# Gated units of a four-layer float32 block: two pairs of column groups as sets of four chunks with 30 block products for 32, and Silu on ScalarE

## The reference

```python
def swiglu(x, w_gate, w_up, w_down):
    return (jax.nn.silu(x @ w_gate) * (x @ w_up)) @ w_down
...
def _swiglu(h, w_gate_up, w_down):
    gu = h @ w_gate_up
    g, u = gu[..., :D_FF], gu[..., D_FF:]
    return (jax.nn.silu(g) * u) @ w_down
```

## Time and profile before

| | |
|---|---|
| median of 3 runs | 1240.11 us (1239.87 to 1241.81) |
| the profiled execution, its own time | 1240.0 us |
| its span, first to last instruction | 1238.2 us |
| TensorE busy | 1225.8 us, 99% of the span |
| VectorE busy | 928.7 us, 75% |
| ScalarE busy | 705.9 us, 57% |
| GpSimd busy | 89.3 us, 7% |
| granted clock of TensorE | 1.00 |

### The profile page before, as it was taken

The page is one execution under the profiler, slowest core; times in us unless marked ns, Lnnn a source line. Parts: engine busy times, 40 slices in busy tenths (PEclk is TensorE's granted clock), DMA queues, the critical chain, the costliest instruction groups (busy, mean ns, idle before and its releaser), DMA issues.

```text
span 1238.2 us, 16107 instructions
## 1 busy us (share of the span) xinstructions
PE 1225.8 (99%) x6318; PEld 1021.4 (82%) x6318; DVE 928.7 (75%) x1293; ACT 705.9 (57%) x1065; POOL 89.3 (7%) x121
## 2 busy tenths in 40 slices
PE   7999999999999999999999999999999999999998
PEld 6778888888888888888888888888888888888887
DVE  7995767698788766778887756676888785666787
ACT  7765654455898644455687535444456644544452
POOL 2410000000100100000232000000001300000000
PEclk9999999999999999999999999999999999999999
DMA  8344545555554565555554224545455315555452
GB/s 308 106 137 148 188 171 204 187 187 203 192 201 159 197 213 197 174 189 212 183 200 170 69 103 169 205 170 204 170 204 187 132 35 204 204 173 199 172 183 89
DMA packets 32539, 216.63 MB, mean 175 GB/s; under 512 B 3904, under 2 KB 4544, under 8 KB 7376
## 3 DMA queue, kind: packets, MB, share of 16 engines
q1 hardware_dynamic: 30384, 210.32, 48.6%
q0 software_dynamic: 1360, 4.78, 1.2%
q10 hardware_dynamic: 720, 0.50, 0.1%
HBM read 214.54 MB, written 1.05 MB: 174 GB/s over the span
## 4 chain that ended last, share of the span: by engine, by line
PE 93%; DVE 4%; issue 1%; DMA 1%; ACT 0%; SPq 0%; DVEq 0%; ACTq 0%
PE PS L484 26%; PE PS L486 26%; PE PS L485 26%; PE PS L490 6%; PE PS L860 2%; PE PS L884 1%; PE PS L521 1%; PE PS L519 1%; PE PS L518 1%; PE PS L567 1%; PE PS L562 1%; PE PS L561 1%; DVE WL L1838 1%; DVE YG L2215 1%; DMA X<-in_x 1%
## 5 line engine op out<-in xcount | busy, mean ns | idle before, releaser
L1838 DVE TENSOR_TENSOR WL<-RAW,WH 128x2048 fp32r<-128x2048 f32 (+3 forms) x200 | 434.1, 2174 | 182.3 <-ACT WH L1199 182.3
L1199 ACT ACTIVATE WH<-RAW 128x2048 fp32r<-128x2048 f32 (+3 forms) x200 | 364.4, 1824 | 262.2 <-PE PS L486 262.1
L484 PE MATMUL PS<-WH,HTh 128*128 128x512 f32 (+1 forms) x848 | 334.6, 395 | 0.8 <-DVE WL L1838 0.6
L486 PE MATMUL PS<-WH,HTl 128*128 128x512 f32 (+1 forms) x848 | 329.0, 388 | 0.0
L485 PE MATMUL PS<-WL,HTh 128*128 128x512 f32 (+1 forms) x848 | 328.3, 387 | 0.0
L486 PEld LDWEIGHTS PS<-WH,HTl 128*128 128x128 f32 x848 | 159.2, 188 | 33.3
L484 PEld LDWEIGHTS PS<-WH,HTh 128*128 128x128 f32 x848 | 159.4, 188 | 32.7 <-DVE WL L1838 1.7
L485 PEld LDWEIGHTS PS<-WL,HTh 128*128 128x128 f32 x848 | 159.5, 188 | 30.6
L484 PE MATMUL PS<-WH,YAh 128*128 128x512 f32 x354 | 139.9, 395 | 0.1
L486 PE MATMUL PS<-WH,YAl 128*128 128x512 f32 x354 | 138.0, 390 | 0.0
L485 PE MATMUL PS<-WL,YAh 128*128 128x512 f32 x354 | 137.8, 389 | 0.0
(11 more groups left out here) (446 smaller groups left out, 1737.6 us busy)
## 6 DMA issues: line engine op xcount, KB each, us to landing
RAW<-in_w SPq DMA_DIRECT2D x196, 1024.0 KB, 4.9
BC<-in_rows POOLq DMA_DIRECT2D x4, 512.0 KB, 4.1
YG<-in_mem POOLq DMA_DIRECT2D x4, 512.0 KB, 5.0
X<-in_x SPq DMA_DIRECT2D x2, 512.0 KB, 5.4
RAW<-in_w SPq DMA_DIRECT2D x4, 256.0 KB, 5.7
BC<-in_s SPq DMA_DIRECT2D x1, 512.0 KB, 11.6
YG<-in_s SPq DMA_DIRECT2D x1, 512.0 KB, 11.9
BB<-in_s SPq DMA_DIRECT2D x1, 512.0 KB, 12.5
```

The costliest lines, as they stand in the source:

```text
L484: e.matmul(out, ah, bh, start=start, stop=False, skip_group_check=joined)
L486: return e.matmul(out, al, bh, start=False, stop=stop, skip_group_check=joined)
L1199: e.activation(WH[:, c % NW, w], RAW[:, c % NR, w], ACT.Copy).then_inc(S.hi, 1)
L1838: e.tensor_tensor(WL[:, c % NW, w], RAW[:, c % NR, w], WH[:, c % NW, w].bitcast(f32), SUB).then_inc(S.lo, 1)
```

## The change

In each unit the pairs 2 and 3, and 6 and 7, become sets of four chunks. A chunk of a set holds two tiles of k for both pairs of column groups (1024 columns). The first and third of a set are plain, eight products each over four banks; the second and fourth have seven products, with sums of weights (from RAW, as in the down projection, but kept in `TGh`, `TGl`, which lie in YB) and sums of activations, made once per unit from the unit's input (`forms`, buffers GSh and GSl). Eight additions per set join the results before the gates of both pairs. Pairs get banks by a table (`BANKS`). The gate function is Silu of ScalarE for Tanh, so VectorE has one instruction per row tile and the factors 0.5 go; an Exp of two columns ends the ScalarE part of the first three units. The order of all three engines around the sets is written anew (`ahead`, `column_set`, `group`). The diff, cut:

```diff
 NF = len(FAST)
+SETS = (2, 6)
+NS = 2 * len(SETS)
+BANKS = ((0, 1), (6, 7), (0, 2), (1, 3), (6, 7), (2, 3), (0, 2), (1, 3), (6, 7), (0, 1), (6, 7))
...
+    def half(k, nk, g):
+        return ("pair", gate, up, lead, k, nk, 256 * g, uo + 256 * g)
     for g in range(11):
-        for k in (0, 4):
-            out.append([("pair", gate, up, lead, k, 4, 256 * g, uo + 256 * g)])
+        if g in SETS:
+            for k in (0, 2, 4, 6):
+                if k in (2, 6):
+                    out.append([half(k, 1, g + 1), half(k, 1, g), half(k + 1, 1, g), half(k + 1, 1, g + 1)])
+                else:
+                    out.append([half(k, 1, g), half(k, 1, g + 1), half(k + 1, 1, g), half(k + 1, 1, g + 1)])
+        elif g - 1 not in SETS:
+            out += [[half(0, 4, g)], [half(4, 4, g)]]
     for ci in range(11):
...
                 out += [sb(key + n, [128, NF, 384], f32r) for n in ("SFh", "SFl")]
...
+        TGh, TGl = (a[:, 0:8, :].rearrange("p (n a) c -> p n (a c)", a=2) for a in (YBh, YBl))
         SR = JK[:, :].rearrange("p (b c) -> p b c", b=2)
...
+        def joined(f, n):
...
+            def early_chunk(f, a, first, c):
+                m, i = FASTS[c], 0 if first else 1
+                GSh, GSl = FB[f][8:10]
+                k = 2 if first else 6
...
+                def mul(b, x, w, own):
+                    return mm3(PS[:, b, :], *x, *w, own and first, not first)
...
+                def top_left():
+                    return mul(5, Y(0, 0), W(1), True)
+                def with_sums():
+                    e.wait_ge(S.tlo, 4 * m + 1)
+                    mul(6, S_(1), T(1), True).then_inc(S.tu, 1)
+                    e.wait_ge(S.tlo, 4 * m + 2)
+                    if first:
+                        e.wait_ge(S.ylo, fold_n(f, a - 2))
+                    mul(4, S_(0), T(0), True).then_inc(S.tu, 1)
+                e.wait_ge(S.lo, c + 4)
+                e.wait_ge(S.gsl, 2 * f + i + 1)
+                if first:
+                    side(0, Y(1, 0), W(2))
+                    side(1, S_(3), W(3))
+                    e.wait_ge(S.an, gt_n(f, a - 1, 1))
+                    with_sums()
+                else:
+                    top_left().then_inc(S.ms, 1)
+                    with_sums()
+                    side(0, Y(1, 0), W(2))
+                    side(1, S_(3), W(3))
+                e.wait_ge(S.tlo, 4 * m + 3)
+                mul(7, S_(2), T(2), True).then_inc(S.tu, 1)
+                e.wait_ge(S.tlo, 4 * m + 4)
+                tk = mul(2, Y(1, 1), T(3), False)
+                if first:
+                    e.wait_ge(S.ylo, fold_n(f, a - 1))
+                    tk = top_left()
+                tk.then_inc(S.used, 1)
+            def set_mm(f, a, cs, folds):
+                def plain(c, k0):
+                    e.wait_ge(S.lo, c + 4)
+                    for t in range(2):
+                        if k0 == 0:
+                            e.wait_ge(S.an, gt_n(f, a - 1 if a > 2 and t else a - 2, 1))
+                        for k in (k0, k0 + 1):
+                            for half in range(2):
+                                o = (k % 2) * 1024 + half * 512
+                                tk = product(c, PS[:, 2 * t + half, :], (HTh, HTl), k, t, slice(o, o + 512), k == 0,
+                                             k == 5 and t == 1 and half == 1)
+                    tk.then_inc(S.used, 1)
+                plain(cs[0], 0)
+                folds()
+                early_chunk(f, a, True, cs[1])
+                plain(cs[2], 4)
+                early_chunk(f, a, False, cs[3])
...
-                edge_mm(cs[0:2], 4, 512, FPAIRS[0], ed)
-                for g in range(1, 11):
-                    def freed(k, t):
-                        if k == 0 and g > 2:
-                            e.wait_ge(S.an, gt_n(f, g - 3, t))
-                    rows_mm(cs[2 * g:2 * g + 2], 4, 8, 512, (HTh, HTl), FPAIRS[g % 3], freed)
-                    fold(g - 1)
+                def free(g, t):
+                    if g - 2 in SETS:
+                        e.wait_ge(S.cb, set_joins(f, g - 2) + (6 if t else 1))
+                    elif g == 5:
+                        e.wait_ge(S.an, gt_n(f, 3, 1))
+                    elif g == 9:
+                        e.wait_ge(S.an, gt_n(f, 7, 1))
+                    elif g == 10:
+                        e.wait_ge(S.an, gt_n(f, 8, t))
+                def group(g):
+                    for n, c in enumerate(cs[2 * g:2 * g + 2]):
+                        e.wait_ge(S.lo, c + 4)
+                        for t in range(2):
+                            if n == 0:
+                                free(g, t)
+                            for k in range(4 * n, 4 * n + 4):
+                                w = slice(512 * (k % 4), 512 * (k % 4) + 512)
+                                tk = product(c, PS[:, BANKS[g][t], :], (HTh, HTl), k, t, w, k == 0, k == 7)
+                        tk.then_inc(S.used, 1)
+                edge_mm(cs[0:2], 4, 512, BANKS[0], ed)
+                group(1)
+                fold(0)
+                set_mm(f, 2, cs[4:8], lambda: fold(1))
+                group(4)
+                fold(2)
+                fold(3)
+                group(5)
+                fold(4)
+                set_mm(f, 6, cs[12:16], lambda: fold(5))
+                group(8)
+                fold(6)
+                fold(7)
+                group(9)
+                fold(8)
+                group(10)
+                fold(9)
                 wide_mm(cs[22:], ed + 1, lambda k: ydst(f, k), lambda ci: e.wait_ge(S.ylo, fold_n(f, 9 if ci == FAST[0] else ci)), lambda: fold(10), 1, f)
...
                 m = FASTS[c]
-                e.wait_ge(S.used, c - 1)
+                dst = TGh if early(c) else TSh
+                e.wait_ge(S.used, c - 4 if early(c) and m % 2 == 0 else c - 1)
                 for q, n in enumerate(T_ORDER):
                     e.wait_ge(S.tr, 4 * m + (2, 3, 3, 4)[q])
-                    copy(TSh[:, n, :], TR_[:, n, :]).then_inc(S.thi, 1)
+                    copy(dst[:, n, :], TR_[:, n, :]).then_inc(S.thi, 1)
...
-                    e.wait_ge(S.used, cs[2 * g + 1] + 1)
+                    p = BANKS[g]
+                    if g in SETS or g - 1 in SETS:
+                        a = g if g in SETS else g - 1
+                    else:
+                        a = None
+                        e.wait_ge(S.used, cs[2 * g + 1] + 1)
                     if g == 0:
-                        e.wait_ge(S.rsx, f + 1)
+                        e.wait_ge(S.rs, RSTD[f"row{ed}"])
                     for t in range(2):
                         if g > 1:
-                            e.wait_ge(S.sg, gt_n(f, g - 2, t))
-                        e.activation(TH[:, g % 2, t, :], PS[:, p[t], 0:256], ACT.Tanh, scale=st[:, 4 + t:5 + t]).then_inc(S.th, 1)
+                            e.wait_ge(S.an, gt_n(f, g - 2, t))
+                        if a is not None:
+                            e.wait_ge(S.cb, set_joins(f, a) + (8 if t else 3 + g - a))
+                        e.activation(TH[:, g % 2, t, :], PS[:, p[t], 0:256], ACT.Silu, scale=st[:, 2 + t:3 + t]).then_inc(S.th, 1)
                 def fold(g):
                     hi, lo, j = ydst(f, 2 * g)
...
+                def forms():
+                    for i in range(2):
+                        e.wait_ge(S.gs, 8 * f + 4 * i + 4)
+                        copy(FB[f][8][:, i, :], (JK[:, 512:1024], FB[f][5][:, 2, :])[i]).then_inc(S.gsh, 1)
+                def group(g, *folds):
+                    feed(cs[2 * g])
+                    feed(cs[2 * g + 1])
+                    for g_ in folds:
+                        fold(g_)
+                    tanh(g)
+                def ahead(a):
+                    g = a - 1
+                    sums_hi(cs[2 * a + 1])
+                    feed(cs[2 * g])
+                    fold(g - 1)
+                    tanh(g)
+                    feed(cs[2 * g + 1])
+                def column_set(a):
+                    feed(cs[2 * a])
+                    fold(a - 1)
+                    sums_hi(cs[2 * a + 3])
+                    feed(cs[2 * a + 1])
+                    n = SETS.index(a)
+                    e.wait_ge(S.ms, 9 * f + 3 * n + 1)
+                    copy(FB[f][5][:, 2, :], PS[:, 5, :]).then_inc(S.eo, 1)
+                    feed(cs[2 * a + 2])
+                    tanh(a)
+                    tanh(a + 1)
+                    feed(cs[2 * a + 3])
                 edge_mm(cs[0:2], ed)
                 tanh(0)
-                for g in range(1, 11):
-                    feed(cs[2 * g])
-                    feed(cs[2 * g + 1])
-                    fold(g - 1)
-                    tanh(g)
-                    if beside:
-                        beside(g)
+                forms()
+                ahead(2)
+                column_set(2)
+                group(4, 2, 3)
+                if beside:
+                    beside(1)
+                    beside(2)
+                ahead(6)
```

(78 more changed lines are left out.)

72 lines of the change are left out of this document (45 added, 27 removed).

## The result

The changed kernel takes 1305.31 us (median of 5 runs, 1304.57 to 1306.2) against 1240.64 for the kernel before: ratio 1.0521, 95% interval 1.0509 to 1.0533. The forecast was 1284, with a range from 1261 to 1300. The sign was right and the size too small by 21 us; 1305 lies outside the range. The span of the profiled execution is 1303.5 us, 65.3 more than before.

The account below looks back on a forecast made before the run. TensorE's matmuls were taken as the bound nearly everywhere (93% of the chain). Waits of 21.4 + 10.3 + 23.5 = 55.2 us less 10.9 gained put 44.3 on 1240.0: 1284, range 1261 to 1300.

Parts of the forecast that it names:

- The gain: Two chunks of each set have seven products for eight: 48 matmuls fewer at 0.227 us, 10.9 us saved.
- VectorE's load: VectorE's busy time about 95 us higher in all; net 24 us a unit into 33 free.
- First wait: Before chunk 4 of each unit, TensorE idle until VectorE's late split: 6.0 us in two units, 4.7 in two, 21.4 together.
- Second wait: Inside chunk 5, `top_left` waits for the rest of pair 1's fold: 2.6 us, 10.3 in four units.
- Third wait: Half way through chunk 12, row tile 1 waits for gate 5: 5.5 us, 1.5 more in the first unit, 23.5 together.
- The clock: TensorE at half pace after the long waits: taken as 0, against 12.4 us; as a rival 1297, chance 0.25.
- paid in full: After the third wait, time lost to a fallen clock would all count; a stretch costs up to 2.8 us.
- the cold start: At the kernel's start, matmuls after idle time come 0.43 us apart until about 13.7: evidence for the clock rival.
- The sum: Whole kernel: 55.2 us lost in three waits, 10.9 gained, 1240.0 + 44.3 = 1284.
- The table switch for Silu before pair 0: ScalarE, each unit: 1.28 us load, costs nothing since Silu ends before VectorE is free; with the drain, 4 us higher.

Follow-up runs that it names:

- the best version: Changed kernel with new order, gates 1 and 5 before sums' rests, activation sums in gaps, pair 4's small fold operations earlier: 1234.04 us, ratio 0.9949 to the kernel before.
- the kernel with filled waits: Changed kernel plus matmuls with unused results where TensorE waits, before chunk 4 and in chunk 12: 1303.05 us, ratio 1.0503 to the kernel before.

## Why the prediction was too low

*The gain.* 48 matmuls fewer (6270 for 6318), as counted. In the best version each unit from its first turn to its last is 1.1, 1.6, 1.6 and 1.6 us shorter, 6.0 in all, out of the 10.9: about 2 are the slower pace of the matmuls on the new sums (0.25 a set, eight sets), 1.8 small waits of 0.6 at most, and some 1.1 I can't place.

*VectorE's load.* "About 95 us higher": 91.7 (928.7 to 1020.4).

*First wait.* Predicted 6.0, 6.0, 4.7, 4.7; measured 5.7, 5.7, 4.4, 4.4. Right, by the mechanism and by the queue worked out step by step: sums of chunk 5 end at 151.1 (150.5 predicted), ScalarE's copies at 152.2 (151.6), and the split of chunk 4 follows them.

*Second wait.* Predicted 2.6 each; measured 1.1 in all. The step itself held: with TensorE at full clock it is 2.1 in every unit (the kernel with filled waits). What failed beside it is the clock, which filled the wait with slow matmuls.

*Third wait.* This is the step that failed: 7.0 and three times 5.5 predicted, 10.0, 8.5, 8.2, 8.2 measured, 34.9 for 23.5. The text has "fold of pair 4 209.4, gate 5 210.3", which prices that fold as one rest of 0.6 us. Pair 4 is one of those whose fold forms sums, 3.7 us, as I had counted for pair 2 in the same sentence, from the earlier trace rows. The 3.1 us missing cover the gap between 5.5 and 8.2 to 8.5; moving the gate ahead of the fold took 3.7 to 4.4 off the wait. The 1.5 added for the first unit was about right: its wait is 1.5 to 1.8 longer than the others, with 0.63 of it from ScalarE's switch to the Silu table (213.24, 1.28 us).

*The clock.* The second failed step: taken as 0, with 12.4 as the bound. The mechanism of that rival was the true one, and the trace after shows 15.3 us of slow matmuls. I had said that after the first wait it would be nearly all taken out of the second, which is what happened, so its net price there is near nothing. After the third it is 1.9 us a unit on average (1.36, 1.36, 2.57 and 2.16), where the bound had 2.8, and 7.5 in all; when the waits were filled 5.3 of these came back, so "paid in full" says somewhat too much. I gave the rival 0.25, because the only row that bore on it was the cold start. A cold start is exactly a start after idle time, and a pause of 5 us that I myself forecast was reason enough to take it as the likely case. The Trainium skill's rule (TensorE: Matmul & The Clock Gate, Why this matters for your kernels), that an idle TensorE falls back to 4/8, held behind all eight long waits.

*The sum.* 1284.3 forecast; third wait + 11.4; slow matmuls after it + 7.5; second wait 10.3 become 1.1 of wait and 7.9 of slow matmuls after the first, - 1.3; first wait - 1.2; pace of the new matmuls and edges of the gaps + 4.7. That makes 1305.4, against 1305.31 measured. The last term is the remainder of the balance, so that the sum closes is no proof of it. With the fold of pair 4 at its 3.7 us, and nothing else changed, the same working would have given some 12 us more, 1297, inside the range; the rest is the clock and the pace.

*The table switch for Silu before pair 0*: hidden, as said. The load at 140.65 takes 1.28 us and the Silu starts at 141.94; the drain of 1380 ns that the Trainium skill counts (ScalarE: Activation LUTs, What ACT_TABLE_LOAD costs) does not show there.

*What I missed altogether* is that the loss was a matter of order. I wrote that "what decides is the order of its queue", and then priced the order as given. ScalarE's copies ahead of the rounding stand in that working with their times; I didn't see that they held up an idle VectorE, and that exchanging them is worth 21.6 us.

## What to carry to other kernels

When an engine off the critical path is filled from 70% to 90%, write its queue and that of the engine that feeds it by due time: first what the bounding engine asks for next, then what it needs a chunk later. Look in the trace for idle time on the engine that is late: closing gaps of 2.9 and 2.5 us of idle VectorE ahead of late splits gave 21.6 us, taking work off it none. Moving one item in such a queue can hand the wait to the next (+3 us here) or give back part of what it takes (-7 and -22), and all together gave -71; so judge an order as a whole. An optimisation that measures nothing (Silu, 1240.7 for 1240.3) can still be what makes a later one pay (8.7 us). Whether this order is the best one, or whether GpSimd would help in the last version, was not tried.
